# Values of the dilated attention projected with tokens on the partitions, and a different order of the opening loads and matmuls

## The chip, the cores and the metric

One core of one Trainium2 chip runs the whole kernel. The metric is the device time of one execution in microseconds, the median of three runs. Every time below is in microseconds unless ns is written.

## The reference, cut to what matters

A decoder trunk of two layers over 512 tokens with 1024 channels, all in float32. Layer 0 mixes tokens with three groups of dilated window attention, layer 1 with differential attention. Each layer then has a squared-ReLU MLP and a gated embedding. The part that the change touches is the projection of layer 0:

```python
def dilated_mixture_attention(h, w_qkv, w_o, rel_table):
    B, T, _ = h.shape                      # T = 512, D_MODEL = 1024
    qkv = (h @ w_qkv).reshape(B, T, N_GROUPS_A, 3, HEADS_A, HEAD_DIM)   # 3 groups, q/k/v, 16 heads, 64
    outs, lses = [], []
    for g, (window, dilation) in enumerate(DIL_CONFIGS):    # (128,1), (512,4), (2048,16)
        o, l = dilated_group_attention(qkv[:, :, g, 0], qkv[:, :, g, 1], qkv[:, :, g, 2],
                                       window, dilation, rel_table)
        outs.append(o)
        lses.append(l)
    alpha = jax.nn.softmax(jnp.stack(lses, axis=0), axis=0)
    o = jnp.sum(alpha[..., None].astype(h.dtype) * jnp.stack(outs, axis=0), axis=0)
    return o.reshape(B, T, D_MODEL) @ w_o
```

`h` is `rmsnorm(x, norm_mix[0])`; the factor of a token, one over its root mean square, can be applied after the projection.

## The kernel before

**Units.** TensorE's work is cut into units. A unit is one block of 128 weight columns against 1024 inputs and all 512 tokens. Weights and activations are each split into a high and a low part (type fp32r), and a product is three matmuls per chunk of 128 inputs: high by high (line 1455), low by high (1456), high by low (1457). So a unit is 8 chunks of 3 matmuls, 24 matmuls with 512 moving columns. The weight block is the stationary operand, the activations move, and the output in PSUM (`unit_out`, two banks in turn) has channels on the partitions and tokens along the row. Unit u uses weight buffer u % 2. SyncE loads a block to `w_raw` once ScalarE and VectorE have split the block before last; ScalarE writes `w_hi` (line 755) when TensorE has finished with that buffer, VectorE writes `w_lo` (1035), and TensorE waits for it (`lo_done`). VectorE takes each product out of PSUM and scales it per token (line 1197, `rstd` or `rstd_q`), counted in `evac_done`.

**Stage A** is layer 0's projection and attention. It goes over 8 pairs of heads in 9 steps of 9 slots. In step s, slot i projects unit i of pair s (`A_ORDER`), while the attention of pair s-1 runs beside it in the same slots: scores at slots 0 and 2, the softmax parts on VectorE and ScalarE, transposes of the probabilities at slots 6 and 8, and the products with the values at slot 8 (`values_a`). The steps alternate between two halves (par 0 and 1) of the buffer `heads`. Steps 1 to 6 are a loop of two steps per turn.

**Values.** The product of probabilities and values needs the values with tokens on the partitions. So each of the three V units (slots 0, 1, 2) is written out as `a_v_t` and then turned: after the unit of the next slot TensorE makes four 128x128 transposes to the bank `misc` (line 1531), and ScalarE copies it to `heads` (line 847). That is 24 turns over the 8 pairs.

**The outset.** SyncE's queue loads the four parts of x, then weight blocks 0 and 1, then `selector` (33 rows). TensorE turns x in eight chunks (`turn_x`, four transposes each; chunks 2c and 2c+1 need part c of x); VectorE copies each from PSUM to `h_a` (1074), ScalarE makes its high part (763), VectorE its low part (1050). Six turns (`AHEAD`) are issued before unit 0's first chunk, the others among its chunks. ScalarE and VectorE place the splits of weights 0 and 1, and four sums of squares (802), between those chunks. From chunk 4 on, two chunks of unit 1 follow each chunk of unit 0. Then comes one matmul that spreads the token factors over the partitions (the spread, 1644), and then four fp32 matmuls of the bias table with `selector` (the bias vectors, 1652, banks of `logits` and `turned`), which ScalarE copies to `vec_sb` (858). VectorE's list after the spread factors is: split weights 2, copy the spread (1092), make `rstd_q` (1094), take out unit 0. Then TensorE makes the turn of slot 1 and unit 2.

Of the kernel before, what the change touches and what calls it, by code (L numbers as in the profile page):

```python
# [38 lines left out]
P = 128  # L39
T = 512  # L40
# [18 lines left out]
A_ORDER = [(0, V), (1, V), (2, V), (0, Q), (0, K), (1, Q), (1, K), (2, Q), (2, K)]  # L59
A_UNITS = len(A_ORDER)  # L60
# [51 lines left out]
AHEAD = 6  # L112
# [104 lines left out]
def build(nc, x, p, rel_bias, a_w_qkv, a_w_o, b_w_qkv, b_w_o, lq1, lk1, lq2, lk2, subln, norm_mix,  # L217
          norm_mlp, w_ff1, w_ff2, norm_ple, w_gate, w_proj, final_norm, selector, out):
    ctx = ExitStack()
    with ctx:  # L220
# [105 lines left out]

        def end_sums(hf):

            return (attn, unit_out[(U_END - 1) % 2])[hf][:, 0:NH]
# [34 lines left out]
        def a_v_t(i):  # L364

            return (scaled, hidden)[i % 2][:, :]

# [78 lines left out]
        vec_ready = sem("vec_ready")  # L446
# [23 lines left out]
        v_ready = sem("v_ready")  # L470
        scores_ready = sem("scores_ready")
# [100 lines left out]
        def _(sp):  # L572
# [9 lines left out]
            for c in range(NT):  # L582
                load_x(c)

            def load(u, src):

                par = u.const % 2
                wait_apart(sp, lo_done, u - 1, (s_sel, 16))
                sp.dma_start(w_raw[par][:, 0:min(KC, width_of(u)), :], src
                             ).then_inc(raw_ready[par], 16)  # L590
# [3 lines left out]
            def load_a(pair, u, i):  # L594
                g, kind = A_ORDER[i]
                load(u, wa[:, :, bass.ds((pair.times(P) + (g * 3 + kind) * D).v, P)])
# [43 lines left out]
            for u in range(2, A_PAIRS * A_UNITS):  # L640
                load_a(At(u // A_UNITS), At(u), u % A_UNITS)
                if u == 3:
                    sp.wait_ge(vec_ready, 4)
                    sp.dma_start(vectors.ap(), vec_sb).then_inc(vectors_ready, 16)
# [100 lines left out]
        def _(sc):  # L745
# [50 lines left out]

            def start_squares(r):
# [10 lines left out]
            for n in range(KC):  # L808
# [4 lines left out]
                if n in (2, 4, 5, 6):  # L813
                    start_squares((2, 4, 5, 6).index(n))
# [4 lines left out]
            def sub_a(s, par, i, has_proj, has_attn):  # L819
# [21 lines left out]
                if has_proj and i in (4, 5):  # L841

                    split_qk_hi(a_parts(par, A_ORDER[i - 1][1]), a_product(i - 1), u)
                if has_proj and 1 <= i <= GROUPS:

                    wait(sc, vt_ps, s.times(GROUPS) + i)
                    sc.activation(a_buf(par, i - 1, V), misc[:, :], ACT.Copy).then_inc(v_ready, 1)  # L847
# [5 lines left out]
                if start:  # L853
                    for c in range(4):
                        cols = min(T, VEC - c * T)
                        bank = (logits, turned)[c % 4 // 2][0:HEADS, c % 2 * T:c % 2 * T + cols]
                        sc.wait_ge(vec_ps, c + 1)
                        sc.activation(vec_sb[:, c * T:c * T + cols], bank, ACT.Copy
                                      ).then_inc(vec_ready, 1)
# [74 lines left out]
            def sub_b(s, par, i, has_proj, has_scores, has_prev, has_norm):  # L934
# [30 lines left out]
                if has_scores and i == 0:  # L965
                    wait(sc, vt_ps, s + GROUPS * A_PAIRS)
# [62 lines left out]
        def _(ve):  # L1029
# [23 lines left out]
            def statistics(norm):  # L1053
# [3 lines left out]
                if norm == 3:  # L1057
# [10 lines left out]
            ve.wait_ge(s_table, 16)  # L1068
            ve.tensor_scalar(table[0:NB, :], table[0:NB, :], -1.0, None, ALU.mult
                             ).then_inc(table_ready, 1)  # L1070
            for n in range(KC + 1):
# [5 lines left out]
                if n in (2, 4):  # L1077
                    split_lo(At(n // 2 - 1))

            def start_statistics():  # L1080
# [9 lines left out]
                split_lo(At(2))  # L1090
# [3 lines left out]
                ve.tensor_scalar(rstd_q[:, :], rstd[:, :], -SCALE, None, ALU.mult  # L1094
                                 ).then_inc(rstd_q_ready, 1)
                ve.wait_ge(rstd_q_ready, 1)
# [22 lines left out]
            def sub_a(s, par, i, has_proj, has_attn):  # L1119
# [64 lines left out]
                if has_proj and i in (4, 5):  # L1184
                    split_qk_lo(a_parts(par, A_ORDER[i - 1][1]), a_product(i - 1), s.times(2) + (i - 3))
                if has_proj:
                    if start:
                        start_statistics()
                    g, kind = A_ORDER[i]
                    dst = a_v_t(i) if kind == V else a_buf(par, g, kind)  # L1190
                    if g == 0 and kind != V:
                        dst = a_product(i)
# [14 lines left out]
                if start:  # L1207
                    ve.wait_ge(s_lam, 16 * 4)
                    for n in range(2):
                        ve.tensor_tensor_reduce(  # L1210
                            out=hidden[:, 0:E], in0=lam_in[:, 2 * n, :], in1=lam_in[:, 2 * n + 1, :],
# [240 lines left out]
        def _(te):  # L1452
# [140 lines left out]

            def sub_a(s, par, i, has_proj, has_attn):
# [33 lines left out]
                if has_proj:  # L1628
                    start = s.reg is None and s.const == 0 and i < 2
                    if not start:  # L1630
                        whole(u, IN[0])
                    elif i == 0:
                        for n in range(KC):
# [9 lines left out]
                        te.wait_ge(start_diagonals, 1)  # L1643
                        te.matmul(attn[:, :], ones[:, :], square[0][:, :], start=True, stop=True
                                  ).then_inc(stat_ps, 1)
                        te.wait_ge(table_ready, 2)
                        te.wait_ge(x_copied, KC)
                        te.wait_ge(s_sel, 16)
                        for c in range(4):
                            cols = min(T, VEC - c * T)  # L1650
                            wait(te, vec_ready, c - 3)
                            te.matmul((logits, turned)[c % 4 // 2][0:HEADS, c % 2 * T:c % 2 * T + cols],
# [237 lines left out]
```

## Time and profile before

| | |
|---|---|
| median of 3 runs | 1652.12 (1651.77 to 1654.23) |
| profiled execution | 1652.47, its span 1650.7 |
| TensorE (PE) busy | 1622.1, 98% of the span |
| weight loads (PEld) busy | 1332.5, 81% |
| VectorE / ScalarE / GpSimd busy | 921.8 / 608.0 / 59.6 |
| DMA | 159.66 MB, mean 97 GB/s |

In the profile a matmul's busy time overlaps with that of the next, so the pace of a stream is read from the starts of its matmuls, not from their durations. In a line of the timeline the numbers ahead are the start and the duration, `xN` the number of instructions that are merged in it, and the bracket the idle time of that engine before it with what ended it.

### The profile page before, as it was taken

What the parts mean: (1) busy time and instruction counts of PE and PEld (TensorE: products, weight loads), DVE (VectorE), ACT (ScalarE), POOL (GpSimd) and SP (SyncE); (2) the same over time, 40 slices, a digit from 0 to 9 for tenths busy, and PEclk for the clock granted to TensorE, in tenths of its full rate; (3) what the DMA queues carried; (4) which work ended last, traced back from release to release, by engine and by line L of the source; (5) the groups of instructions that cost most, each with busy time, mean ns of one, the idle gap of its engine ahead of it and who ended that gap; (6) DMA issues with size and microseconds to landing.
All of it is one profiled execution on the core that took longest, in us unless ns stands there. A gap on an engine that the chain in (4) does not pass through costs nothing.

```text
span 1650.7 us, 22246 instructions
## 1 busy us (share of the span) xinstructions
PE 1622.1 (98%) x8323; PEld 1332.5 (81%) x8323; DVE 921.8 (56%) x1632; ACT 608.0 (37%) x1058; POOL 59.6 (4%) x58
## 2 busy tenths in 40 slices
PE   7999999999999899999999999999999999999998
PEld 5888888888888688888888878888868888888887
DVE  5454554554555763545455676777776354545555
ACT  5234234234233432222223444665553122222344
POOL 0000000000000200000001110000020000000111
PEclk9999999999999999999999999999999999999999
DMA  5543443443332233333333332323223333333332
GB/s 142 145 121 90 109 121 88 109 120 83 97 85 69 83 96 102 89 102 93 99 98 92 105 113 77 90 63 98 58 74 102 101 91 102 89 102 89 102 102 78
DMA packets 308312, 159.66 MB, mean 97 GB/s; under 512 B 31156, under 2 KB 303085, under 8 KB 308254
## 3 DMA queue, kind: packets, MB, share of 16 engines
q1 hardware_dynamic: 308092, 158.85, 34.0%
q8 instruction: 37, 0.61, 0.2%
q14 instruction: 21, 0.17, 0.0%
q10 hardware_dynamic: 162, 0.03, 0.0%
HBM read 156.64 MB, written 10.60 MB: 101 GB/s over the span
## 4 chain that ended last, share of the span: by engine, by line
PE 94%; DVE 3%; ACT 1%; POOL 1%; DMA 1%; issue 0%; SPq 0%; POOLq 0%; ACTq 0%
PE unit_out L1455 28%; PE unit_out L1457 27%; PE unit_out L1456 27%; PE turned L1531 2%; PE attn L1589 2%; PE attn L1816 1%; PE logits L1455 1%; PE misc L1531 1%; PE logits L1531 1%; POOL sumsq L740 1%; PE logits L1457 1%; PE logits L1456 1%; DMA w_raw<-in_a_w_qkv_dram 1%; PE logits L1571 1%; DVE act_lo L1050 1%; DVE heads L1242 0%
## 5 line engine op out<-in xcount | busy, mean ns | idle before, releaser
L1455 PE MATMUL unit_out<-act_hi,w_hi 128*128 128x512 f32 (+1 forms) x2032 | 805.6, 396 | 11.7 <-DVE act_lo L1050 8.9
L1457 PE MATMUL unit_out<-act_hi,w_lo 128*128 128x512 f32 (+1 forms) x2032 | 790.9, 389 | 0.0
L1456 PE MATMUL unit_out<-act_lo,w_hi 128*128 128x512 f32 (+1 forms) x2032 | 790.3, 389 | 0.0
L1455 PEld LDWEIGHTS unit_out<-act_hi,w_hi 128*128 128x128 f32 x2032 | 382.4, 188 | 100.8 <-DVE act_lo L1050 9.9
L1457 PEld LDWEIGHTS unit_out<-act_hi,w_lo 128*128 128x128 f32 x2032 | 381.7, 188 | 79.8
L1456 PEld LDWEIGHTS unit_out<-act_lo,w_hi 128*128 128x128 f32 x2032 | 382.2, 188 | 77.4 <-issue 2.4
L755 ACT ACTIVATE w_hi<-w_raw 128x1024 fp32r<-128x1024 f32 (+3 forms) x259 | 274.0, 1058 | 440.5 <-PE unit_out L1457 362.9
L1035 DVE TENSOR_TENSOR w_lo<-w_raw,w_hi 128x1024 fp32r<-128x1024 f32 (+3 forms) x259 | 324.0, 1251 | 104.9 <-ACT w_hi L755 104.9
L896 ACT ACTIVATE act_hi<-hidden 128x512 fp32r<-128x512 f32 x64 | 40.5, 633 | 243.4 <-DVE hidden L1261 243.4
L740 POOL TENSOR_TENSOR sumsq<-sumsq,square 128x512 f32<-128x512 f32 x41 | 57.5, 1403 | 1576.0 <-ACT square L776 1574.3
L1258 DVE TENSOR_TENSOR scaled<-unit_out,rstd 128x512 f32<-128x512 f32 x64 | 44.1, 690 | 67.7 <-PE unit_out L1457 67.7
L1103 DVE TENSOR_TENSOR h_a<-h_a,unit_out 128x512 f32<-128x512 f32 x40 | 27.5, 688 | 91.7 <-PE unit_out L1457 91.7
L1103 DVE TENSOR_TENSOR heads<-heads,unit_out 128x512 f32<-128x512 f32 x40 | 27.5, 687 | 80.7 <-PE unit_out L1457 80.7
L838 ACT ACTIVATE probs<-probs,w_raw 128x256 f32<-128x256 f32 (+1 forms) x128 | 61.9, 485 | 28.2 <-DVE w_raw L1128 27.3
L1264 DVE TENSOR_TENSOR act_lo<-hidden,act_hi 128x512 fp32r<-128x512 f32 x64 | 44.3, 692 | 44.7 <-ACT act_hi L896 44.7
L1197 DVE TENSOR_TENSOR scaled<-unit_out,rstd 128x512 f32<-128x512 f32 x24 | 16.6, 692 | 57.8 <-PE unit_out L1457 57.8
L1261 DVE SCALAR_TENSOR_TENSOR hidden<-scaled 128x512 f32<-128x512 f32 x64 | 44.3, 692 | 2.2
L1339 DVE CUSTOM_DVE_ANT_0 probs<-logits,bias 128x512 f32<-128x512 f32 (+3 forms) x64 | 28.8, 487 | 15.6 <-PE logits L1457 15.6
L1197 DVE TENSOR_TENSOR heads<-unit_out,rstd 128x512 f32<-128x512 f32 x16 | 11.1, 691 | 47.2 <-PE unit_out L1457 47.2
L955 ACT ACTIVATE probs<-probs,low 128x512 f32<-128x512 f32 (+3 forms) x64 | 35.3, 553 | 3.4 <-DVE low L1339 3.4
L847 ACT ACTIVATE heads<-misc 128x512 f32<-128x512 f32 x24 | 14.3, 598 | 58.0 <-PE misc L1531 58.0
L763 ACT ACTIVATE act_hi<-heads,gains 128x512 fp32r<-128x512 f32 x24 | 17.3, 722 | 49.4 <-DVE heads L1103 25.6
(231 smaller groups left out, 1152.6 us busy)
## 6 DMA issues: line engine op xcount, KB each, us to landing
w_raw<-in_w_ff_dram SPq DMA_DIRECT2D x128, 512.0 KB, 4.0
w_raw<-in_a_w_qkv_dram SPq DMA_DIRECT2D x72, 512.0 KB, 3.8
w_raw<-in_b_w_qkv_dram SPq DMA_DIRECT2D x24, 512.0 KB, 5.1
w_raw<-in_w_ple_gate_dram SPq DMA_DIRECT2D x16, 512.0 KB, 4.1
bias_tiles_b<-bias_vectors SPq DMA_DIRECT2D x16, 256.0 KB, 4.3
bias<-bias_tiles_b SPq DMA_DIRECT2D x8, 512.0 KB, 3.8
w_raw<-in_a_w_o_dram SPq DMA_DIRECT2D x8, 448.0 KB, 3.7
w_raw<-in_b_w_o_dram SPq DMA_DIRECT2D x8, 384.0 KB, 3.4
```

What stands on the lines that cost most here:

```text
L740: pool.tensor_tensor(sumsq[:, :], sumsq[:, :], square[n % 2][:, :], ALU.add).then_inc(sumsq_done, 1)
L755: sc.activation(w_hi[par][:, 0:width, :], w_raw[par][:, 0:width, :], ACT.Copy).then_inc(hi_done, 1)
L838: e = sc.activation(probs[i][:, cols], probs[i][:, cols], ACT.Exp, bias=low_col, scale=-1.0, accum_out=sum_col)
L1035: ve.tensor_tensor(w_lo[par][:, 0:width, :], w_raw[par][:, 0:width, :], w_hi[par][:, 0:width, :], ALU.subtract).then_inc(lo_done, 1)
L1103: ve.tensor_tensor(h[:, n, :], h[:, n, :], unit_out[u.const % 2][:, :], ALU.add).then_inc(evac_done, 1)
L1258: ve.tensor_tensor(scaled[:, :], unit_out[u.const % 2][:, :], rstd[:, :], ALU.mult).then_inc(evac_done, 1)
L1261: ve.scalar_tensor_tensor(hidden[:, :], scaled[:, :], 0.0, scaled[:, :], ALU.max, ALU.mult).then_inc(hid_ready, 1)
L1264: ve.tensor_tensor(MID[layer][1][:, n, :], hidden[:, :], MID[layer][0][:, n, :], ALU.subtract).then_inc(hid_done, 1)
L1455: te.matmul(bank, w_k[0], hi, start=start, stop=False)
L1456: te.matmul(bank, w_k[0], lo, start=False, stop=False)
L1457: return te.matmul(bank, w_k[1], hi, start=False, stop=stop)
L1531: last = te.transpose(bank[:, dst:dst + P], src, ident[:, :])
```

## The change

- Groups 1 and 2 of the values are projected with the activations as the stationary operand (128 tokens) and the weights moving (256 columns, two pairs of heads at once). The output has the tokens on the partitions, and VectorE takes it out with the factor `start_scale` of its token straight to `heads`; there is no turn and no copy on ScalarE. Such work is two units (halves of the 1024 inputs) with 48 matmuls of 256 columns each, over both banks of `unit_out`. Its four units per two pairs stand in slots 0 to 3 of the odd steps.
- Group 0's values are made and turned as before, at slot 1 of the even steps and slot 5 of the odd ones.
- To even out the slots, an even step also makes group 0's and group 1's Q of the next pair.
- Outset: the loads go x0, x1, weights 0, selector, x2, weights 1, x3. `AHEAD` is 4. The bias-vector matmuls stand behind the chunks 1 to 4 of unit 0, in the banks `attn` and `misc`, two of them copied out by ScalarE and two by VectorE, at fixed places of their lists. The spread stands between unit 0's last chunk and unit 1's last two. VectorE scales the table after chunk 0, and splits weights 2 and makes `rstd_q` after it has taken out unit 0. The lambda sums move to slot 2 of step 0.

```diff
-A_ORDER = [(0, V), (1, V), (2, V), (0, Q), (0, K), (1, Q), (1, K), (2, Q), (2, K)]
+A_ORDER = ([(0, V, 0), (0, Q, 0), (0, K, 0), (1, Q, 0), (1, K, 0), (2, Q, 0), (2, K, 0), (0, Q, 1), (1, Q, 1)],
+           [(1, V, 0), (1, V, 1), (2, V, 0), (2, V, 1), (0, V, 0), (0, K, 0), (1, K, 0), (2, Q, 0), (2, K, 0)])
+A_TURN_V = [order.index((0, V, 0)) + 1 for order in A_ORDER]
+KV = KC // 2
-AHEAD = 6
+AHEAD = 4
...
+        def vec_part(c):
+            cols = min(T, VEC - c * T)
+            return (attn, misc)[c % 2][0:HEADS, 0:cols], slice(c * T, c * T + cols)
+        def a_values(g, half):
+            pairs = heads[:, :].rearrange("p (par x t) -> p par x t", par=2, t=T)
+            return pairs[:, :, g * 3 + V, half * BLK:(half + 1) * BLK].rearrange("p h (a c) -> p a h c", c=P)
+        def wide_weights(w):
+            return w[:, 0:KC, :].rearrange("p (k n) c -> p k (n c)", n=2)
...
+                g, kind, n = A_ORDER[pair.const % 2][i]
+                if kind == V and g:
+                    first = (g * 3 + kind) * D + (pair.const - 1) * P
+                    load(u, wa[:, n * KV:(n + 1) * KV, first:first + 2 * P], wide_weights(w_raw[u.const % 2]))
...
+            load_x(0)
+            load_x(1)
             load_a(At(0), At(0), 0)
+            sp.dma_start(sel_sb, selector).then_inc(s_sel, 16)
+            load_x(2)
             load_a(At(0), At(1), 1)
-            sp.dma_start(sel_sb, selector).then_inc(s_sel, 16)
+            load_x(3)
...
+            def vec_out(c):
+                bank, cols = vec_part(c)
+                sc.wait_ge(vec_ps, c + 1)
+                sc.activation(vec_sb[:, cols], bank, ACT.Copy).then_inc(vec_even, 1)
...
                 slab_hi(n, n, h_a, IN[0])
                 if n in (1, 3):
                     split_hi(At(n // 2))
-                if n in (2, 4, 5, 6):
-                    start_squares((2, 4, 5, 6).index(n))
+                if n in (2, 4):
+                    vec_out(n - 2)
+                if n > 3:
+                    start_squares(n - 4)
...
                 if n in (2, 4):
                     split_lo(At(n // 2 - 1))
+                if n == 1:
+                    ve.wait_ge(s_table, 16)
+                    ve.tensor_scalar(table[0:NB, :], table[0:NB, :], -1.0, None, ALU.mult
+                                     ).then_inc(table_ready, 1)
+                if n in (4, 6):
+                    bank, cols = vec_part(n - 3)
+                    ve.wait_ge(vec_ps, n - 2)
+                    ve.tensor_copy(vec_sb[:, cols], bank).then_inc(vec_odd, 1)
...
-                split_lo(At(2))
                 ve.wait_ge(stat_ps, 1)
                 ve.tensor_copy(rstd[:, :], attn[:, :]).then_inc(rstd_ready, 1)
...
+                        for n in range(2):
+                            if n == 0:
+                                wait(ve, values_half, (s - 1).half().times(GROUPS - 1) + g)
+                            else:
+                                wait(ve, units_done, u + 1)
+                            bank = unit_out[(u.const - 1 + n) % 2]
+                            ve.tensor_tensor(
+                                a_values(g, n),
+                                bank[:, :].rearrange("p (a h c) -> p a h c", a=2, h=2),
+                                start_scale[:, 2 * n:2 * n + 2].unsqueeze(2).unsqueeze(3).to_broadcast([P, 2, 2, P]),
+                                ALU.mult).then_inc(evac_done, 1)
...
                 if start:
+                    split_lo(At(2))
+                    ve.tensor_scalar(rstd_q[:, :], rstd[:, :], -SCALE, None, ALU.mult
+                                     ).then_inc(rstd_q_ready, 1)
...
+            def vectors_of(c):
+                if c == 0:
+                    te.wait_ge(table_ready, 2)
+                    te.wait_ge(gains_ready, 1)
+                    te.wait_ge(s_sel, 16)
+                elif c > 1:
+                    te.wait_ge((vec_even, vec_odd)[c % 2], 1)
+                bank, cols = vec_part(c)
+                te.matmul(bank, table, sel_sb[:, cols], start=True, stop=True).then_inc(vec_ps, 1)
+            def values_unit(u, g, kind, half):
+                w = u.const % 2
+                wait(te, lo_done, u + 1)
+                for a in range(NT):
+                    bank = unit_out[(u.const - half + a // 2) % 2][:, a % 2 * BLK:(a % 2 + 1) * BLK]
+                    if half == 0 and a % 2 == 0:
+                        wait(te, evac_done, u - 1 + a // 2)
+                    for k in range(KV):
+                        hi, lo = (x[:, half * KV + k, a * P:(a + 1) * P] for x in IN[0])
+                        w_k = [wide_weights(x[w])[:, k, :] for x in (w_hi, w_lo)]
+                        te.matmul(bank, hi, w_k[0], start=half == 0 and a % 2 == 0 and k == 0, stop=False)
+                        te.matmul(bank, hi, w_k[1], start=False, stop=False)
+                        last = te.matmul(bank, lo, w_k[0], start=False,
+                                         stop=half == 1 and a % 2 == 1 and k == KV - 1)
+                    if half == 1 and a == 1:
+                        last.then_inc(values_half, 1)
+                last.then_inc(units_done, 1)
...
                             if n == KC - 1:
                                 last.then_inc(units_done, 1)
+                                te.wait_ge(start_diagonals, 1)
+                                te.wait_ge(vec_even, 2)
+                                te.matmul(attn[:, :], ones[:, :], square[0][:, :], start=True, stop=True
+                                          ).then_inc(stat_ps, 1)
+                            if 0 < n <= 4:
+                                vectors_of(n - 1)
                             if n >= KC // 2:
                                 k = 2 * n - KC
                                 last = unit(At(1), IN[0], act_ready, part=(k, k + 2))
...
-                if has_proj and 1 <= i <= GROUPS:
+                if has_proj and i == A_TURN_V[par]:
                     wait(te, evac_done, u)
```

## Rows read from the trace of the kernel before

**Rows 1.** The page: busy time of each engine.
```profile
PE 1622.1 (98%) x8323; PEld 1332.5 (81%) x8323; DVE 921.8 (56%) x1632; ACT 608.0 (37%) x1058; POOL 59.6 (4%) x58
```
**Rows 2.** The waits of TensorE: total, times, longest.
```profile
PE unit_out L1455 <- DVE act_lo L1050: 8.9, 8, 2.1
```
**Rows 3.** Windows: stretch, its length, busy time of each engine, granted clock, DMA.
```profile
135.00:500.00 365.00, 365.00 (x2259) 304.40 (x2258) 193.51 (x497) 135.96 (x311) 0.00 (x0) 1.00 0.37 101
```
**Rows 4.** Timeline of TensorE, slots 6 and 7 of step 1, first and past the last.
```profile
112.52 0.48 PE L1455 MATMUL unit_out<-act_hi,w_hi 128*128 128x512 f32 x1
...
123.50 0.82 PE L1531 MATMUL logits<-ident,probs 128*128 128x128 f32 x6
```
**Rows 5.** Timeline of TensorE near the end, the first and last of 58 matmuls.
```profile
1632.96 0.28 PE L1457 MATMUL unit_out<-act_hi,w_lo 128*128 128x256 f32 x1
...
1639.79 0.28 PE L1457 MATMUL misc<-ple_hi,w_lo 128*128 128x256 f32 x1
```
**Rows 6.** Timeline of TensorE around turns and other changes of work in stage A.
```profile
38.73 0.48 PE L1455 MATMUL unit_out<-act_hi,w_hi 128*128 128x512 f32 x1
...
44.30 0.60 PE L1531 MATMUL misc<-ident,scaled 128*128 128x128 f32 x4
44.65 0.48 PE L1455 MATMUL unit_out<-act_hi,w_hi 128*128 128x512 f32 x1
...
84.70 0.60 PE L1531 MATMUL misc<-ident,scaled 128*128 128x128 f32 x4
85.22 1.16 PE L1571 MATMUL logits<-heads 64*128 64x128 f32 x16
...
130.28 0.39 PE L1457 MATMUL unit_out<-act_hi,w_lo 128*128 128x512 f32 x1
130.60 3.50 PE L1589 MATMUL attn<-probs,heads 128*64 128x128 f32 x60
```
**Rows 7.** Timeline of TensorE at the outset.
```profile
7.45 1.97 PE L1531 MATMUL logits<-ident,stage 128*128 128x128 f32 x8
...
15.06 0.50 PE L1455 MATMUL unit_out<-act_hi,w_hi 128*128 128x512 f32 x1 [1.41 <-DVE w_lo L1035]
...
19.98 0.50 PE L1455 MATMUL unit_out<-act_hi,w_hi 128*128 128x512 f32 x1 [1.43 <-DVE act_lo L1050]
...
28.27 1.02 PE L1644 MATMUL attn<-square,ones 128*128 128x512 f32 x2
29.22 1.89 PE L1652 MATMUL logits<-heads,probs 33*16 33x512 f32 x4
...
32.38 0.66 PE L1531 MATMUL misc<-ident,scaled 128*128 128x128 f32 x4
32.79 0.48 PE L1455 MATMUL unit_out<-act_hi,w_hi 128*128 128x512 f32 x1
```
**Rows 8.** Timeline of VectorE at the outset.
```profile
9.09 0.16 DVE L1069 TENSOR_SCALAR probs<-probs 32x16 f32<-32x16 f32 x1 [1.12 <-DMA probs<-in_rel_bias_dram]
9.17 1.27 DVE L1074 COPY h_a<-logits 128x512 f32<-128x512 f32 x2
10.70 0.75 DVE L1050 SCALAR_TENSOR_TENSOR act_lo<-h_a,gains,act_hi 128x512 fp32r<-128x512 f32 x1 [0.26 <-ACT act_hi L763]
...
28.26 1.23 DVE L1035 TENSOR_TENSOR w_lo<-w_raw,w_hi 128x1024 fp32r<-128x1024 f32 x1 [3.33 <-ACT w_hi L755]
...
30.58 0.69 DVE L1197 TENSOR_TENSOR scaled<-unit_out,rstd 128x512 f32<-128x512 f32 x1
```
**Rows 9.** Timeline of ScalarE at the outset.
```profile
9.94 1.33 ACT L763 ACTIVATE act_hi<-h_a,gains 128x512 fp32r<-128x512 f32 x2 [4.81 <-DVE h_a L1074]
...
12.69 1.06 ACT L755 ACTIVATE w_hi<-w_raw 128x1024 fp32r<-128x1024 f32 x1 [1.42 <-DMA w_raw<-in_a_w_qkv_dram]
...
30.29 0.59 ACT L858 ACTIVATE stage<-logits 16x512 f32<-16x512 f32 x1 [2.06 <-PE logits L1652]
```
**Rows 10.** Windows at the outset, columns as in rows 3 (the last two: DMA share, GB/s).
```profile
6.00:8.00 2.00, 0.81 (x4) 0.73 (x5) 0.38 (x2) 0.00 (x0) 0.00 (x0) 1.00 1.04 327
```

More of the change, by code:

```diff
@@ L366, in a_v_t, with a_made, a_splits @@
             return (scaled, hidden)[i % 2][:, :]
+        def a_made(par, i):
+            g, kind, ahead = A_ORDER[par][i]
+            return (par + ahead) % 2, g, kind
+        def a_splits(par, i):
+            return i > 0 and A_ORDER[par][i - 1][0] == 0 and A_ORDER[par][i - 1][1] != V
+        def a_values(g, half):
[3 more added lines that the diff above has]
+            return w[:, 0:KC, :].rearrange("p (k n) c -> p k (n c)", n=2)
         def b_v_t(par):
@@ L580, in load_x, with load @@
                              ).then_inc(s_x[c], 16)
-            for c in range(NT):
-                load_x(c)
-            def load(u, src):
+            def load(u, src, dst=None):
                 par = u.const % 2
                 wait_apart(sp, lo_done, u - 1, (s_sel, 16))
-                sp.dma_start(w_raw[par][:, 0:min(KC, width_of(u)), :], src
+                sp.dma_start(w_raw[par][:, 0:min(KC, width_of(u)), :] if dst is None else dst, src
                              ).then_inc(raw_ready[par], 16)
@@ L852, in sub_a @@
                                   ).then_inc(o_hi_ready, 1)
[L853 to L859, printed above, removed]
+                if s.reg is None and s.const == 0 and i == 2:
                     sc.wait_ge(lam_sums, 2)
@@ L1210, in sub_a @@
                         ve.tensor_tensor_reduce(
-                            out=hidden[:, 0:E], in0=lam_in[:, 2 * n, :], in1=lam_in[:, 2 * n + 1, :],
+                            out=probs_t[:, 0:E], in0=lam_in[:, 2 * n, :], in1=lam_in[:, 2 * n + 1, :],
                             scale=1.0, scalar=0.0, op0=ALU.mult, op1=ALU.add,
@@ L1629, in sub_a @@
                     start = s.reg is None and s.const == 0 and i < 2
-                    if not start:
+                    if A_ORDER[par][i][1] == V and A_ORDER[par][i][0]:
+                        values_unit(u, *A_ORDER[par][i])
+                    elif not start:
                         whole(u, IN[0])
@@ L1642, in sub_a @@
                         last.then_inc(units_done, 1)
[L1643 to L1652, printed above, removed]
-                                      table, sel_sb[:, c * T:c * T + cols], start=True, stop=True
-                                      ).then_inc(vec_ps, 1)
                 elif i < KC - 1:
@@ L1745, in head_squares @@
                 if has_scores:
-                    wait(te, v_ready, s + GROUPS * A_PAIRS)
+                    wait(te, v_ready, s + A_PAIRS)
                 wait(te, osq_ready, s - 1)
```

57 lines of the change are left out of this document (30 added, 27 removed).

## The prediction
> **What bounds the kernel now.** I read the page first, then the waits of TensorE, then windows over stage A, then the timeline of one step and of the outset. The page gives TensorE 1622.1 of 1650.7 [rows 1]. Its waits show no more than single microseconds each: the longest sum for a wait within the projections and MLPs is 8.9, for `act_lo` [rows 2]. In the 365 us from 135 to 500, which lie wholly in stage A, TensorE is never idle, VectorE has 194 and ScalarE 136 of them, and the granted clock is 1.00, the upper of its two levels (2.4 GHz) [rows 3]. So in stage A the time is the sum of what TensorE streams; work taken off VectorE or ScalarE is worth nothing there, and a TensorE instruction removed or added counts in full. The exception is the outset up to the start of unit 2 at 32.79, where TensorE waits 1.41 before chunk 0 and 1.43 before chunk 4 [rows 7]. These are two separate sums.
>
> **Stage A, wider values: what it adds.** Slots 6 and 7 hold 48 matmuls of 512 columns in 10.98 from first start to the next work [rows 4]. A stream that follows fp32 work loses some 0.09 at its start, so the pace is 10.89 / 48 = 0.2269, and a unit takes 5.45. The pace of fp32r matmuls with 256 moving columns, a weight load ahead of each, stands near the end: 57 intervals in 6.83, 0.1198 each [rows 5]. Two of them take 0.2396 for 0.2269: the same columns, one more matmul's fixed part. A half of the wide values has 48, 5.75, and there are 16 halves: 16 x (5.75 - 5.45) = **+4.9**. The nearest rows are the very form (fp32r, 128x128 stationary, 256 columns), so the value is theirs; only the operands change places. Bounds: 0.1134 (half of 0.2269, no fixed part) gives 0, and 0.124 gives 8.1.
> The Trainium skill, "TensorE: Matmul & The Clock Gate", section "Back-to-back issue gap", puts the interval at columns / 2.4 + 2.5 ns. By that rule this term would be an estimated +1.0, for a whole sum of -6.4. The trace does not agree: 119.8 and 226.9 ns are some 13 ns over columns / 2.4, at either width. I go by the trace.
>
> **What it removes.** 24 turns become 8. A slot with a turn that is followed by a unit lasts 5.92, from 38.73 to 44.65; without, 5.45: 0.47, of which 0.35 (44.30 to 44.65) is the transposes and the rest the slower restart [rows 6]. A turn ahead of the scores of slot 2 takes 0.52 (84.70 to 85.22), but without it the entry from a unit to 64-row work costs some 0.09 more than a matmul's pace (0.32 from 130.28 to 130.60) [rows 6]; net 0.43. The turn ahead of the merge of slot 4 I take as that one. Step 0 loses two turns of 0.47 (0.94). Steps 2, 4 and 6 lose 0.47 + 0.43 each (2.7). Steps 1, 3, 5 and 7 lose three, 1.33, and gain one at slot 5 that runs into other transposes, 0.35: 3.9 in all. Sum **-7.5**; at 0.35 a turn it is 5.6, at 0.52 it is 8.3. The 16 ScalarE copies and the better packets of the wide loads are off the path.
>
> **Waits that it could add.** In a first half the second bank is needed after 24 matmuls, 2.9 after the unit before has ended, where a whole unit leaves 5.45. VectorE takes out 512 columns in 0.69 [rows 8] and has nothing but that queued there, so cover is about 2. In a second half VectorE waits for the first two token tiles at 2.9. Ahead of that in its list is the split of the next weights, which needs ScalarE's 1.06 after the unit before and its own 1.23 [rows 8, 9]: 2.3, so it is in time. Next weights are then ready long before the unit ends. I put all of this at 0. The number of takings-out is the same (9 per step). So stage A gives 4.9 - 7.5 = **-2.6**.
>
> **The outset.** Here I follow the lists by hand with these durations: copy 0.64 (1.27 for two), high part 0.68 (1.33 for two), low part 0.70 (0.75 less an overlap of 0.05), split 1.03 and 1.17 (likewise), chunk 0.69 ((28.27 - 19.98) / 12), four bias-vector matmuls 3.16 (0.89, 0.89, 0.89, 0.50 by columns), the spread 0.95 (28.27 to 29.22), a copy of 16 rows 0.59 [rows 7 to 9]. A result is there for another engine about 0.2 after the next matmul could start.
> 1. VectorE no longer waits to 9.09 for the table. Eight transposes take from 7.45 to about 9.2 [rows 7, 8], so the first four are there at 8.5, and copy 0 moves from 9.17 to 8.5.
> 2. Weights 0 have two parts of x (1 MB, 3.2 at 327 GB/s) less ahead of them [rows 10]: they land near 9.5 and ScalarE's wait of 1.42 [rows 9] is gone. High parts 0 and 1, then the split: 10.7 to 11.7. VectorE: copies 0 to 2 and low parts 0 and 1, then its split: 12.2 to 13.4. Chunk 0 starts at 13.4 for 15.06: 1.7 sooner.
> 3. TensorE: chunk 0, a turn, chunk 1, to 15.3; bias vectors 0 to 16.2. ScalarE's copy of them stands ahead of its high part 3 and the split of weights 1. So: copy 16.5 to 17.1, high part 3 to 17.7, split to 18.8. VectorE: its split to 19.9, its copy of bias vectors 1 to 20.6, copy 5 to 21.2, low part 4 to 21.9. The early start is lost: chunk 4 starts at 21.9 for 19.98 [rows 7]. Four squares, now all behind this, still end near 28.
> 4. From there TensorE is full: 12 chunks 8.2, the last bias vectors 0.5, the spread 0.95, three restarts 0.3: 31.9. Before, the chunks ended at 28.27, and spread and bias vectors lasted to 32.38.
> 5. The spread ends at 30.5; copy and taking out unit 0 last to 32.0 on VectorE. The turn could be done by 32.4. But the split of weights 2, which was done in the shade of the spread (28.26), now stands behind the taking out: 32.0 to 33.2. Unit 2 starts at 33.2 for 32.79: **+0.4**.
> Bounds: if the bias-vector copies delay nothing, chunk 4 starts at about 20.0 and step 4 ends near 30.0; unit 2 then starts near 31.4, -1.4. If weights 0 or the selector land as late as weights 0 did (12.69 and after), chunk 0 is back at 15 and everything is some 1.5 later: +1.9. The lambda sums, now at slot 2 of step 0, come after unit 2 is taken out (33.2 + 5.45 + 0.2 + 0.69 = 39.6) and ahead of ScalarE's split of weights 4. No row here prices them; I allow 2.0, so that split ends at 42.7 and VectorE's at 43.9, wanted at 44.1: 0, with at most 1 if they take 3.
>
> **Sum.** -2.6 + 0.4 = -2.2. The profiled execution took 1652.47 (its span 1650.7 and 1.8 around it), 0.35 above the median of the runs; from the median I forecast **1649.9**. Its own range is 1648.4 to 1651.8.
>
> **Rivals.**
> A. *The outset gains* (chance 0.17). The two copies of bias vectors fall into gaps of ScalarE, which waits often there, and TensorE's idle 2.8 [rows 7] takes up most of the bias matmuls. Against it: step 3, where ScalarE stands waiting with high part 3 behind it. Time: -2.6 - 1.4 = -4.0, 1648.1.
> B. *Matmuls of 256 columns cost half of those of 512* (0.07). For it: a stream with the same stationary operand twice in a row, in the order high, high, low. Against it: rows 5 had that too. Term 0 for 4.9: -7.5 + 0.4, 1645.0. The rule named above lies beside this case.
> C. *Slower* (0.08). Loading a new stationary operand of activations ahead of every 256 columns does not hide as behind 512, for the weight loads are busy 81% of the span at half that rate of loads [rows 1]. It decides above 0.1227, where 768 matmuls use up the -2.2 (768 x 0.0029); at 0.13 it gives +7.8 more, a total of +5.6, 1657.7. Against it: rows 5 hold it at 0.1198 with a load each.
> D. *No change to speak of* (0.16): the outset is 1.5 to 2 worse through late landings, and the gain of stage A pays for it: 1651.5 to 1652.
>
> My case has 0.52. No change means within 0.2%, 3.3 us, about what a measurement of this kernel can tell. Faster takes B, most of A, and a little of mine where turns save 8.3: 0.28. Slower is C with a little of D: 0.09. Same is the rest, 0.63. The range 1647.3 to 1653.0 takes in my case, A and D and leaves out B and C, 0.15.
>
> **What would show it.** In the changed profile: 256-column matmuls of `unit_out` 0.120 apart in slots 0 to 3 of the odd steps, and no idle of TensorE there; 32 transposes to `misc` from `scaled` and none from `hidden`; chunk 0 near 13.4, chunk 4 near 21.9 with some 1.5 idle ahead of it released by `act_lo`; unit 2 near 33.2, released by `w_lo`. Wrong would be: another interval than 0.120; waits of TensorE for `evac_done` in the wide units; ScalarE not waiting for the bias vectors ahead of high part 3; a unit in slots 3 to 5 of step 0 held by the lambda sums.

## The result, and the profile after

The changed kernel takes 1658.43 (median of 9 runs, 1655.95 to 1661.85); the kernel before took 1652.04 in the same session (9 runs). The ratio is 1.0037, 95% interval 1.0027 to 1.0047: slower by 6.1, where 1649.9 was forecast and a range that ended at 1653.0. The profiled execution took 1660.3 (span 1658.5), 7.8 more than that of before. Three slow executions in the whole study (3598 of the kernel before, 7346 in experiment 6, 3099 in experiment 11) are left out of all ratios and medians below.

The waits of TensorE in the changed kernel, against [rows 2]:

```profile
PE unit_out L1512 <- DVE act_lo L1088: 9.1, 9, 2.1
PE misc L1593 <- DMA probs<-in_b_subln_dram: 7.5, 1, 7.5
PE logits L1621 <- issue: 5.1, 2, 2.8
...
PE logits L1588 <- DMA stage<-in_x_dram: 1.2, 1, 1.2
...
PE unit_out L1512 <- DVE w_lo L1073: 0.5, 1, 0.5
```

The third row is new. "issue" means that TensorE waited for nothing that the profile shows, twice, on the first matmul of a step in stage A (the scores, line 1621). The page's DMA queues have one new number too:

```profile
q1 hardware_dynamic: 299900, 158.85, 33.6%
q8 instruction: 57, 0.93, 0.2%
```

Before, the page had 37 packets on the queue that loads instructions, and between 200 and 440 us none. Now 15 fall in that stretch. The timeline gives the start of each step of stage A as the first scores on TensorE:

```profile
72.97 0.33 PE L1621 MATMUL logits<-qk_hi 64*128 64x128 f32 x2
...
135.22 0.33 PE L1621 MATMUL logits<-qk_hi 64*128 64x128 f32 x2
...
198.67 0.33 PE L1621 MATMUL logits<-qk_hi 64*128 64x128 f32 x2 [2.36 <-issue]
...
262.42 0.33 PE L1621 MATMUL logits<-qk_hi 64*128 64x128 f32 x2
...
326.31 0.33 PE L1621 MATMUL logits<-qk_hi 64*128 64x128 f32 x2 [2.79 <-issue]
...
390.04 0.33 PE L1621 MATMUL logits<-qk_hi 64*128 64x128 f32 x2
...
451.08 0.33 PE L1621 MATMUL logits<-qk_hi 64*128 64x128 f32 x2
```

Before, every step lasted 61.95 or 61.96 (72.08, 134.03, 195.98, ...). The two idle stretches stand where step 3 and step 5 begin. TensorE's stage A is a loop over pairs of steps (1 and 2, 3 and 4, 5 and 6), so these are its two jumps back. In this execution each loses more than its idle time. Behind the first:

```profile
199.22 0.29 PE L1621 MATMUL logits<-qk_lo_a,qk_hi 64*128 64x256 f32 x2
...
200.66 0.42 PE L1675 MATMUL unit_out<-w_lo,act_hi 128*128 128x256 f32 x1
200.87 0.41 PE L1676 MATMUL unit_out<-w_hi,act_lo 128*128 128x256 f32 x1
...
203.43 0.41 PE L1676 MATMUL unit_out<-w_hi,act_lo 128*128 128x256 f32 x1
203.65 0.32 PE L1674 MATMUL unit_out<-w_hi,act_hi 128*128 128x256 f32 x1
203.81 0.28 PE L1675 MATMUL unit_out<-w_lo,act_hi 128*128 128x256 f32 x1
203.92 0.28 PE L1676 MATMUL unit_out<-w_hi,act_lo 128*128 128x256 f32 x1
```

TensorE was idle for 2.36, worked at the full pace for some 1.6 from 198.67 on, and then the granted clock fell: it is 0.50 in each window from 200.5 to 203.5 and 1.00 from 204 on. There the matmuls of 256 columns stand 0.213 apart and afterwards 0.12: 1.2 GHz for 3.4 us, then 2.4 GHz again. The whole account against before, by the starts of the steps (after minus before): +0.89 at step 1, +1.19, then +2.69 (the stall), +4.49 (the slow stretch), +6.42, +8.20, +7.29 and +7.57 at step 8. Unit 2 alone was +1.89.

### The profile page after: what moved, and what is told of

It is laid out like the page before. It is cut to its first block, busy times and chain, and to the rows that moved or that the text cites. A ratio compares the mean times of both kernels' runs of the same rounds, so it can differ in the third digit from the quotient of the medians.

```text
span 1658.5 us, 22831 instructions
## 1 busy us (share of the span) xinstructions
PE 1624.2 (98%) x8643; PEld 1347.3 (81%) x8643; DVE 924.1 (56%) x1634; ACT 599.6 (36%) x1040; POOL 59.6 (4%) x58
## 4 chain that ended last, share of the span: by engine, by line
PE 94%; DVE 3%; ACT 1%; POOL 1%; issue 1%; DMA 0%; ACTq 0%; POOLq 0%
PE unit_out L1512 26%; PE unit_out L1514 25%; PE unit_out L1513 25%; PE unit_out L1674 2%; PE unit_out L1675 2%; PE unit_out L1676 2%; PE turned L1588 2%; PE attn L1646 2%; PE attn L1900 1%; PE logits L1512 1%; PE logits L1588 1%; POOL sumsq L775 1%; DVE act_lo L1088 1%; DVE heads L1299 1%; PE logits L1628 1%
## 5 line engine op out<-in xcount | busy, mean ns | idle before, releaser
L1512 PE MATMUL unit_out<-act_hi,w_hi 128*128 128x512 f32 (+1 forms) x1904 | 754.5, 396 | 11.1 <-DVE act_lo L1088 9.1
L1514 PE MATMUL unit_out<-act_hi,w_lo 128*128 128x512 f32 (+1 forms) x1904 | 740.5, 389 | 0.0
L1513 PE MATMUL unit_out<-act_lo,w_hi 128*128 128x512 f32 (+1 forms) x1904 | 739.8, 389 | 0.0
L1512 PEld LDWEIGHTS unit_out<-act_hi,w_hi 128*128 128x128 f32 x1904 | 358.0, 188 | 97.1 <-DVE act_lo L1088 11.8
L1674 PE MATMUL unit_out<-w_hi,act_hi 128*128 128x256 f32 x256 | 74.3, 290 | 0.0
L1675 PE MATMUL unit_out<-w_lo,act_hi 128*128 128x256 f32 x256 | 73.3, 286 | 0.0
L1676 PE MATMUL unit_out<-w_hi,act_lo 128*128 128x256 f32 x256 | 73.2, 286 | 0.0
L1674 PEld LDWEIGHTS unit_out<-w_hi,act_hi 128*128 128x128 f32 x256 | 50.1, 196 | 1.1 <-issue 0.2
L1675 PEld LDWEIGHTS unit_out<-w_lo,act_hi 128*128 128x128 f32 x256 | 50.1, 196 | 0.0
L1676 PEld LDWEIGHTS unit_out<-w_hi,act_lo 128*128 128x128 f32 x256 | 50.0, 195 | 0.0
```

Of the source, the lines that this page charges most:

```text
L1512: te.matmul(bank, w_k[0], hi, start=start, stop=False)
L1513: te.matmul(bank, w_k[0], lo, start=False, stop=False)
L1514: return te.matmul(bank, w_k[1], hi, start=False, stop=stop)
L1674: te.matmul(bank, hi, w_k[0], start=half == 0 and a % 2 == 0 and k == 0, stop=False)
L1675: te.matmul(bank, hi, w_k[1], start=False, stop=False)
L1676: last = te.matmul(bank, lo, w_k[0], start=False, stop=half == 1 and a % 2 == 1 and k == KV - 1)
```

## The experiments

All ratios are to the kernel before in the same session, five rounds each. Instruction counts are counted in the built program: the body of TensorE's stage-A loop has some 1624 instructions before and some 1778 in the changed kernel.

**1. The changed kernel, TensorE's stage A written out without a loop.**

```diff
-            with eng.Fori(0, (A_PAIRS - 2) // 2) as it:
-                step(At(1, it, 2), 1, True, True)
-                step(At(2, it, 2), 0, True, True)
+            if unrolled:
+                for s in range(1, A_PAIRS - 1):
+                    step(s, s % 2, True, True)
```

> The changed kernel with TensorE's loop over stage A written out (steps 1 to 6 one after the other; the other engines keep their loops). Fetch theory: the two idle stretches of TensorE of 2.4 and 2.8 us at the head of the loop come from instructions that have to be fetched again after the jump back, and each is followed by 3.4 us of half clock (some 1.7 lost). Without a jump back both go: 8.5 us less than the changed kernel's profiled 1660.3, so near 1651.8; the idle 'issue' time ahead of the scores falls from 5.1 to under 0.5 and the clock stays at the upper level through stage A. Dependency theory (TensorE waits at the step's head for something another engine makes late, in the new order of units): the stretches stay, the time stays near 1658.

1652.26, ratio 1.0004 (0.9995 to 1.0013). The "issue" row is gone and stage A runs at the full clock. Between 200 and 440 us 13 instruction packets still come in, and TensorE never stands idle for them: what stalls is not the loading as such but the jump back.

**2. The same edit on the kernel before.**

> The kernel before with TensorE's loop over stage A written out in the same way. Fetch theory: the loop's body was short enough to stay in the instruction memory (no instruction fetch on the DMA rings during turns 2 and 3), so nothing is gained: 1652, within 0.1%. A theory that every jump back costs something would have 0.5 to 1 us less.

1652.43, ratio 1.0003 (0.9994 to 1.0011). Writing the loop out gives nothing where nothing stalled, so what it gave back in 1, 5.5 by the two ratios, is the stalls.

**3. and 4. Either half of the change alone.** `values_only` has the wide values and the outset of before; `outset_only` has the new outset and the units of before.

> The new order of units and the wide values alone, with the opening of the kernel before. Fetch theory: TensorE's body is as long as in the changed kernel, so the stalls are there: +8.5 for them, -2.6 for the work in stage A, 1658. If stalls come from the outset's shift of where the body lies in the instruction blocks, they may be fewer. Dependency theory: the same stalls, as the order is the same. The comparison of this one with the changed kernel gives the outset.

1659.11, ratio 1.0046 (1.0033 to 1.0059).

> The new opening alone, with the units of the kernel before. By the changed kernel's trace, unit 2 starts at 34.7 for 32.8: +1.9, so 1653.9, and no stall at the loop's head (fetch theory: the body has its old length). If the outset were the cause of the stalls, they would be here: 1660.

1655.49, ratio 1.0017 (1.0009 to 1.0026), 1.6 more than expected. The stalls come with the units (4.8 of "issue" in two waits), not with the outset, which shows none.

**5. and 6. The kernel before, padded.** No work is added, only waits in each slot that were satisfied long ago. With N = 19 the built program has 170 more instructions in the body (some 1794), with N = 9 it has 80 more (some 1704); the pages count 510 and 240 more over the three turns. Nothing ahead of the loop differs, so its head lies where it lay before.

```diff
+                    if s.reg is not None:
+                        for _ in range(N):
+                            te.wait_ge(const_ready, 5)
```

> The kernel before, with 19 waits that are long satisfied put into each slot of TensorE's stage-A loop: the body grows from some 1624 to 1794 instructions of TensorE and from 7 to 8 blocks of 256, with no work added. Instruction refetch: the two jumps back now each cost an idle stretch of 2.4 to 2.8 us at the loop's head and 3.4 us at the lower clock behind it, about +8 (1660), and instruction packets appear between 200 and 440 us. If the stalls come from the wide units themselves (their banks, their weight loads): no idle stretch at the head, and 1652.4 plus at most what 20 satisfied waits a slot cost where TensorE's queue runs dry, under 1.

1662.53, ratio 1.0055 (1.0042 to 1.0068). The timeline of TensorE, and windows of it (busy times, then the granted clock):

```profile
135.05 0.33 PE L1564 MATMUL logits<-qk_hi 64*128 64x128 f32 x2
...
199.40 0.47 PE L1564 MATMUL logits<-qk_hi 64*128 64x128 f32 x2 [2.32 <-issue]
...
328.75 0.33 PE L1564 MATMUL logits<-qk_hi 64*128 64x128 f32 x2 [2.30 <-issue]
```

```profile
75.00:199.30 124.30, 122.08 (x756) 101.64 (x754) 64.17 (x162) 45.71 (x104) 0.00 (x0) 1.00 0.39 107
199.50:202.90 3.40, 3.40 (x26) 3.08 (x27) 1.70 (x9) 0.46 (x3) 0.00 (x0) 0.50 0.03 5
```

The stall stands at the same two places, in a kernel that has none of the change, with the granted clock at 0.50 behind it and 56 instruction packets on its page. So neither banks nor weight loads of the wide units make it. The slow stretch behind the first stall lasts 6.8 here, up to 206.2, and step 3 is 3.1 longer by it (65.01 for 61.95).

> As the padded one, but with 9 waits a slot: some 1704 instructions, still 7 blocks of 256. If what counts is whether the body's blocks fit, no stall and 1652.4 (within 0.1%). If each added instruction has its price, half of what the full padding costs, some +4.

1662.60, ratio 1.0058 (1.0046 to 1.0071), "issue" 6.5 in two waits. Both expectations missed: half the padding costs as much as the whole. It isn't a price for each instruction but a threshold, and with the head where it falls in this kernel it lies between 1624 and 1704 instructions. The second stall of this trace has no slow stretch behind it:

```profile
327.92 0.33 PE L1564 MATMUL logits<-qk_hi 64*128 64x128 f32 x2 [3.12 <-issue]
...
330.09 0.40 PE L1457 MATMUL unit_out<-act_hi,w_lo 128*128 128x512 f32 x1
330.32 0.40 PE L1455 MATMUL unit_out<-act_hi,w_hi 128*128 128x512 f32 x1
```

The matmuls of 512 columns stand 0.23 apart, the granted clock is 1.00, and step 5 lasts 61.98. The second stall of experiment 3 (2.39) is like that too, and step 5 lasts its plain 62.24. Of the eight stalls in the four traces, five are followed by a slow stretch of 3.4, one by 6.8 and two by none.

**7. The changed kernel, its loop's head at the start of a block of 256 instructions.**

```diff
-            with eng.Fori(0, (A_PAIRS - 2) // 2) as it:
+            with nc.Fori(0, (A_PAIRS - 2) // 2, engines=[eng.engine],
+                         head_slot={eng.engine: 0}) as it:
```

> The changed kernel with TensorE's stage-A loop kept, but its head placed at the start of a block of 256 instructions, so that its some 1778 instructions touch 7 blocks instead of 8. If the number of blocks touched decides: no stall at the jumps back, no half clock, 1652.3 as with the loop unrolled. If it is the length of the body whatever its place: 1658.4 as the changed kernel.

1651.88, ratio 1.0001 (0.9991 to 1.0010). The body still has some 1778 instructions, more than the 1704 that stalled in 6. So length alone doesn't decide: with nothing but the head's place changed the stalls are gone. The number of blocks touched fits all runs. 1778 from a block's start touch 7 (7 x 256 = 1792). Unplaced, 1624 touch 7 if the head lies no more than 168 behind a block's start, and 1704 touch 8 if it lies more than 88 behind. Its page shows 39 instruction packets, for 57, and none between 200 and 440 us. Its steps:

```profile
72.59 0.33 PE L1623 MATMUL logits<-qk_hi 64*128 64x128 f32 x2
...
134.80 0.33 PE L1623 MATMUL logits<-qk_hi 64*128 64x128 f32 x2
...
195.83 0.33 PE L1623 MATMUL logits<-qk_hi 64*128 64x128 f32 x2
...
258.07 0.33 PE L1623 MATMUL logits<-qk_hi 64*128 64x128 f32 x2
```

**8. and 9. The wide values, the outset of before, and no stalls**, once with the loop written out as in 1, once with the loop placed as in 7.

> The wide values with the outset of before, and TensorE's stage A written out without a loop. By the sum for stage A (wider matmuls +4.9, turns -7.5) 2.6 under the kernel before: 1649.8, ratio 0.9984. If the sum for stage A was wrong and the outset cost nothing: 1652.4.

1650.28, ratio 0.9987 (0.9979 to 0.9996).

> The wide values, the outset of before, and TensorE's stage-A loop kept but with its head at the start of a block of 256 instructions. By the block theory no stall at the jumps back and the same gain as with the loop written out: 1650.0 (ratio 0.9986). If the gain of the written-out version came from having no loop at all, 1652 or more.

1650.59, ratio 0.9988 (0.9979 to 0.9997). Both beat both kernels, the one before by some 2.

**10. The new order of loads alone on the kernel before.**

```diff
-            for c in range(NT):
-                load_x(c)
+            load_x(0)
+            load_x(1)
             load_a(At(0), At(0), 0)
-            load_a(At(0), At(1), 1)
             sp.dma_start(sel_sb, selector).then_inc(s_sel, 16)
+            load_x(2)
+            load_a(At(0), At(1), 1)
+            load_x(3)
```

> The kernel before with the new order of loads alone (x 0, x 1, weights 0, selector, x 2, weights 1, x 3). Theory L, the load order costs: the small loads on ScalarE's queue, on which TensorE's first transposes wait, land at 8 to 9.6 for 7.2 as in all four profiles with the new outset so far (7.5, 9.0, 9.6, 8.3), and x 2 and x 3 late; 1653.5 to 1654.5. Theory P, the placement of the copies and splits costs and the loads only help: small loads at 7.2, weights 0 no longer waited for by ScalarE, chunk 4 at 19.5 or sooner, 1651.5 to 1652.4.

1654.60, ratio 1.0010 (1.0001 to 1.0019), nearer to theory L. Its timeline, TensorE:

```profile
8.42 0.32 PE L1537 MATMUL misc<-ident,probs 57*128 57x57 f32 x1 [8.42 <-DMA probs<-in_b_subln_dram]
...
15.17 0.66 PE L1532 MATMUL turned<-ident,stage 128*128 128x128 f32 x4 [1.60 <-DMA stage<-in_x_dram]
...
20.52 0.50 PE L1456 MATMUL unit_out<-act_hi,w_hi 128*128 128x512 f32 x1 [1.49 <-DVE act_lo L1051]
...
33.34 0.72 PE L1456 MATMUL unit_out<-act_hi,w_hi 128*128 128x512 f32 x1
33.85 0.63 PE L1457 MATMUL unit_out<-act_lo,w_hi 128*128 128x512 f32 x1
34.28 0.63 PE L1458 MATMUL unit_out<-act_hi,w_lo 128*128 128x512 f32 x1
```

TensorE begins at 8.42, for 7.19 before, because the small loads on ScalarE's queue land later. Over all profiles of this study its wait for them is 7.5, 9.0, 9.6, 8.3, 7.9 and 8.4 in the six kernels with the new order (mean 8.5), and 7.2, 7.8, 7.2, 7.2, 6.7, 6.7, 7.2 and 7.2 in the eight with the old (mean 7.2).

That does not explain the whole loss. Unit 2 starts at 33.34 here, and at 32.06 to 32.79 (mean 32.33) in the seven traces with the outset of before: the loads account for 0.6 to 1.3 of this trace. Step 1 starts 2.1 later than before (74.19 for 72.08), and the other 1.5 is a stretch at 1.2 GHz just behind unit 2's start, where the matmuls above stand 0.43 apart; the granted clock of the window from 32 to 36 is 0.68. A stretch like it stands at 32.0 in the trace of `before_padded`, whose outset is untouched, so it need not come from the loads.

**11. The new outset with the loads in the order of before** (the edit of 10 taken back in `outset_only`).

> The new outset (bias-vector matmuls, copies and spread placed among the chunks, split of weights 2 behind the taking-out of unit 0, lambda sums later) with the loads in the order of before. Theory L: small loads at 7.2; what is left is less than half of the outset's 3.1, 1652.4 to 1653.5. Theory P: chunk 0 near 15, chunk 4 near 23, unit 2 near 34.7, 1654.5 or more.

1661.05, ratio 1.0040 (1.0026 to 1.0055), from five runs that lie far apart (1656.3 to 1663.6). Small loads at 7.2, as theory L said, but the time is far above its range. It lies in that of theory P (1654.5 or more), but unit 2, at 42.46 for 34.7, does not. Timeline and windows of TensorE:

```profile
14.77 0.79 PE L1470 MATMUL unit_out<-act_hi,w_hi 128*128 128x512 f32 x1 [3.61 <-DVE w_lo L1044]
...
42.46 0.50 PE L1470 MATMUL unit_out<-act_hi,w_hi 128*128 128x512 f32 x1 [0.47 <-DVE w_lo L1044]
```

```profile
14.80:33.90 19.10, 19.10 (x41) 9.17 (x42) 8.70 (x13) 7.97 (x14) 0.00 (x0) 0.50 0.24 62
```

The new outset turns 4 blocks of x and one more ahead of chunk 0, before it was 6 and one more (`AHEAD`). With weights 0 behind all of x, TensorE stands idle for 3.61, for 1.41 before, and afterwards runs at 1.2 GHz for 19.1 us although the profile shows it busy throughout them (the granted clock had fallen at 13.6, within the idle stretch). Unit 2 starts at 42.46. So the new placement was slower with the old order (1.0040) than with the new one (1.0017); that the idle stretch brought the slow one is argued from this one trace, not shown.

**12. The new outset, the split of weights 2 put back ahead of the spread.**

```diff
+                split_lo(At(2))
                 ve.wait_ge(stat_ps, 1)
...
-                    split_lo(At(2))
```

> The new outset whole, but with VectorE's split of weights 2 put back ahead of its wait for the spread, where it was before. By the outset's step 5 unit 2 waits for this split (0.48 idle at 34.2 in the changed kernel); with it done in the shade of the spread, unit 2 can start when the turn's bank allows, about 1.0 sooner: 1654.5, against 1655.5 with the new outset. If the split does not bound unit 2, 1655.5 stays.

1654.18, ratio 1.0013 (1.0004 to 1.0021), for 1.0017 of the new outset whole. The size is as expected, but the intervals overlap, so the time alone does not show it. The timeline shows the wait for `w_lo` gone and unit 2 bound by the turn ahead of it (this execution took 1656.46, above the median; the whole outset is late in it, for the granted clock was 0.84 from 12 to 16 and 0.73 from 16 to 20). The wait has moved rather than gone: VectorE now splits weights 2 (33.17 to 34.40, once ScalarE's `w_hi` is there) before it copies the spread and takes out unit 0, and TensorE waits 1.54 for that, where it waited 0.47 for `w_lo` in `outset_only`:

```profile
35.78 0.66 PE L1547 MATMUL misc<-ident,scaled 128*128 128x128 f32 x4 [1.54 <-DVE scaled L1209]
36.19 0.47 PE L1471 MATMUL unit_out<-act_hi,w_hi 128*128 128x512 f32 x1
```

## Why the prediction was wrong, point by point

**The step that failed is "Waits that it could add" ... "I put all of this at 0".** It looked for waits on banks and semaphores, and asked nothing about the instructions themselves. The change writes some 154 more instructions of TensorE into the loop body (in four units of each pair of steps two matmuls of 256 columns stand where one of 512 stood; four turns fewer take a little back), and the longer body could no longer be jumped back to without a wait. In the profiled execution the two jumps cost 2.4 and 2.9 of idle time, each with 1.5 of slow clock behind it, by the step lengths of the changed kernel: 63.45, 63.75, 63.89 and 63.73, where 61.03 and 62.24 stood without stalls (experiment 7). That is 2.42 + 1.51 + 2.86 + 1.49 = 8.3. In the medians it is 9.6 with the outset of before (experiment 3 against 9: 1.0046 and 0.9988) and 5.5 to 6 with the new one (1.0037 against 1.0004 and 1.0001); the nine runs of the changed kernel spread over 5.9. Part of that spread may be the slow stretches, 1.5 each, which follow some stalls and not others (experiments 5 and 6). Experiments 1, 2, 5, 6 and 7 show the cause, the length and place of the loop's body: the stalls come without the work and go without removing any. That instructions are fetched anew is read from the packets of that queue (37, 57, 56 and 39 in before, changed, padded and placed; between 200 and 440 us none, 15, 15 and none). The Trainium skill, "Runtime: NRT & Kernel Launch", section "Instruction fetch mechanics", says that the instruction buffer is refilled in blocks of 16 KiB (256 instructions), that TensorE's holds 2048, and that a taken branch whose target lies outside the current window of two blocks must wait for a DMA fetch before execution goes on. The traces agree on the size of the packets (15 for 0.25 MB) and on a stall at the jump. They do not agree on the window: the kernel before jumps back over some 1624 instructions, more than two blocks, without a stall and without a packet. Nor do 2048 instructions fit the runs as read in experiment 7, where bodies that touch 7 blocks turned without a stall and those that touch 8 did not. The measurement decides. I had read nothing of it into the forecast; it should have been a rival with a place of its own.

**Stage A's sum was right.** Wide matmuls, changed kernel:

```profile
74.80 0.28 PE L1675 MATMUL unit_out<-w_lo,act_hi 128*128 128x256 f32 x1
...
80.55 0.28 PE L1675 MATMUL unit_out<-w_lo,act_hi 128*128 128x256 f32 x1
```

48 intervals in 5.75, 0.1198, the value of [rows 5] to the digit; rivals B and C had needed another. The steps of experiment 7 last 62.21 and 62.24 (odd) and 61.03 (even), against 61.95 before. Forecast were +1.22 - 0.98 = +0.25 for an odd step (a quarter of 4.9 and of 3.9) and -0.90 for an even one (a third of 2.7); measured are +0.27 and -0.92. Step 0 gives -1.0: the lag of +1.89 at unit 2 is +0.89 at step 1, for the two turns of 0.94. By the lengths of the steps the term is so -2.7. No wide unit waited for a bank, and the lambda sums held nothing up; one wide unit waited 0.6 for `w_lo` in the trace of experiment 9, whose weights had landed late. By the ratios of experiments 8 and 9 the term is -2.0 to -2.1 for -2.6, and their intervals allow -0.7 to -3.5.

The rule of columns / 2.4 + 2.5 ns that the prediction sets beside this term stands in the Trainium skill, "TensorE: Matmul & The Clock Gate", section "Back-to-back issue gap", for an isolated matmul and not for a stream with a weight load ahead of each, so it was no rule for these rows. With its +1.0 the whole sum would be 1.0 - 7.5 + 0.4 = -6.1; the prediction has -6.4, a slip that no other number rests on.

**The turns** are as forecast: 32 transposes from `scaled`, none from `hidden`.

```profile
L1674 PE MATMUL unit_out<-w_hi,act_hi 128*128 128x256 f32 x256 | 74.3, 290 | 0.0
...
L1588 PE MATMUL misc<-ident,scaled 128*128 128x128 f32 x32 | 4.8, 274 | 0.1
```

**The outset had the right order of events and the wrong size**, +1.9 in this trace for +0.4. This is the second step that failed: in experiments 1 and 7, without the stalls, it alone uses up the gain of stage A. TensorE, against [rows 7]:

```profile
12.70 1.11 PE L1588 MATMUL logits<-ident,stage 128*128 128x128 f32 x4 [1.25 <-DMA stage<-in_x_dram]
13.93 0.80 PE L1512 MATMUL unit_out<-act_hi,w_hi 128*128 128x512 f32 x1
...
16.90 1.03 PE L1660 MATMUL attn<-heads,probs 33*16 33x512 f32 x2
...
23.27 0.50 PE L1512 MATMUL unit_out<-act_hi,w_hi 128*128 128x512 f32 x1 [0.86 <-DVE act_lo L1088]
...
34.68 0.50 PE L1512 MATMUL unit_out<-act_hi,w_hi 128*128 128x512 f32 x1 [0.48 <-DVE w_lo L1073]
```

ScalarE behind the bias vectors, against [rows 9]:

```profile
17.96 0.59 ACT L836 ACTIVATE stage<-attn 16x512 f32<-16x512 f32 x1 [5.12 <-PE attn L1660]
18.46 0.71 ACT L798 ACTIVATE act_hi<-h_a,gains 128x512 fp32r<-128x512 f32 x1
19.07 1.04 ACT L790 ACTIVATE w_hi<-w_raw 128x1024 fp32r<-128x1024 f32 x1
```

VectorE at the end of it, against [rows 8]:

```profile
32.08 0.69 DVE L1134 COPY rstd<-attn 128x512 f32<-128x512 f32 x1 [1.70 <-PE attn L1731]
32.80 0.69 DVE L1249 TENSOR_TENSOR scaled<-unit_out,rstd 128x512 f32<-128x512 f32 x1
33.41 1.22 DVE L1073 TENSOR_TENSOR w_lo<-w_raw,w_hi 128x1024 fp32r<-128x1024 f32 x1
```

The chain is the one of steps 3 to 5: ScalarE waits for the bias vectors with high part 3 behind it, chunk 4 waits for `act_lo`, unit 2 for `w_lo`. It runs 0.5 late at chunk 0 (13.93 for 13.4) and 1.4 to 1.6 late from then on: the first bias vectors at 16.90 for 15.3, the copy at 17.96 for 16.5, chunk 4 at 23.27 for 21.9, unit 2 at 34.68 for 33.2. Two terms were missing from steps 2 and 3. A turn stands ahead of chunk 0 that needs x 2, and x 2, now behind weights 0 and the selector, keeps TensorE idle for 1.25 (I had priced what comes sooner and not what comes later). Behind that idle stretch chunk 0 is slow: its matmuls stand 0.42 apart up to 15.38 for 0.227. That is the distance of the lower clock, but the granted clock reads 1.00 there, so the reason for the slow pace is not shown:

```profile
12.70:15.40 2.70, 2.58 (x8) 1.79 (x9) 2.70 (x5) 0.14 (x1) 0.00 (x0) 1.00 0.83 230
```

A third term is in none of the steps: the small loads, 1.3 later on average with this order, though only 0.3 in this trace. Unit 2 starts at 34.28, 34.68, 35.04 and 35.66 in the four traces with the whole new outset, 2.6 later on average than in the seven with the old one. In the medians the outset costs 2.8 (1.0017). The new order of loads alone costs 1.7 (1.0010, interval 0.2 to 3.1), and not all of that need be the loads (experiment 10). My bound above of +1.9, for late landings, was itself too low.

**The range** left out these cases: rival D priced an outset 1.5 to 2 worse, against a gain that stage A would keep. The mechanism that decided was neither D's nor C's.

## What to carry to other kernels

Before a change that adds instructions inside a hardware loop, count the engine's instructions in the body: a change that wins on every matmul can lose more at the jump back, and the place of the loop's head or writing the loop out took that away here at no cost that could be measured (1.0001 and 1.0004). A wait of "issue" on the first instruction of a loop together with packets on the instruction queue is how it looks in a profile. When loads are put in another order, price what lands later, small loads on other queues too, as carefully as what lands sooner.

## What the runs showed that was not expected

Half the padding stalled as much as all of it: 6.5 of "issue" at 1704 instructions, 4.6 at 1794. Of eight stalls of 2.3 to 3.3, five were followed by 1.2 GHz for 3.4 us, one by 6.8 and two by none, and an idle stretch of 3.61 in the outset by 1.2 GHz for 19.1 us of unbroken work. Stretches of 3.4 stand in the first 40 us of some traces too (experiments 5, 10 and 12) and not of others, and at 1.5 each they blur a comparison of single traces. What starts and ends them stays open, and so does why the small loads land later when x 2, weights 1 and x 3 are issued behind the selector: no run took either apart. Where in a block the unplaced loop begins was not read, and no run put a body of more than 7 blocks at a block's start; that seven blocks fit and eight don't is inferred from five bodies of four lengths.
